# The first root's scaling of the rows on GpSimd instead of VectorE, in a two-layer RWKV-7 / HGRN2 trunk

## The reference, cut to what matters

```
x = x + rms_norm(out, norm_post[0])        # out: RWKV's output projection
h = rms_norm(x, norm_pre[1])
q, f_logit, i, z = split(h @ w_in, 4)      # HGRN2's input projection

def rms_norm(x, w):
    return x * rsqrt(mean(x * x, axis=-1) + NORM_EPS) * w
```

## Time and profile before

| | us |
|---|---|
| median of three runs | 2852.39 |
| lowest, highest | 2851.09, 2854.86 |
| profiled execution, its own time | 2853.62 |
| its span in the trace | 2851.8 |
| PE busy | 2730.1 |
| DVE busy | 1608.9 |
| ACT busy | 1259.1 |
| POOL busy | 138.4 |

### The profile page before, as it was taken

One profiled execution on the slowest core, in us unless ns is written; L12 is line 12 of the kernel. 1 busy time (PEld: TensorE's weight loads), 2 busy tenths in 40 slices (PEclk: granted clock), 3 DMA queues, 4 the chain that ended last, 5 costly groups with the idle time before them and its releaser, 6 DMA issues. The chain is left out here.

```text
span 2851.8 us, 82517 instructions
## 1 busy us (share of the span) xinstructions
PE 2730.1 (96%) x36816; PEld 2567.6 (90%) x36816; DVE 1608.9 (56%) x2679; ACT 1259.1 (44%) x1869; POOL 138.4 (5%) x116
## 2 busy tenths in 40 slices
PE   6999999999999999999889988999999999999997
PEld 5899999999998887888779978999999999999997
DVE  7335313313326777888742267776777767775224
ACT  5345323324414555555532255444544455444222
POOL 0000000000001111010000003000000000000000
PEclk8999999999999999999999999999999999999999
DMA  3333333333311111112132242222333223243322
GB/s 126 108 106 113 109 113 113 113 111 134 115 69 52 50 53 54 51 53 71 43 111 89 90 155 73 95 95 94 97 100 107 95 80 114 95 139 137 124 89 102
DMA packets 86816, 273.48 MB, mean 96 GB/s; under 512 B 16448, under 2 KB 29504, under 8 KB 65984
## 3 DMA queue, kind: packets, MB, share of 16 engines
q1 hardware_dynamic: 77248, 250.37, 26.5%
q10 hardware_dynamic: 9216, 17.83, 1.7%
HBM read 221.63 MB, written 46.54 MB: 94 GB/s over the span
## 5 line engine op out<-in xcount | busy, mean ns | idle before, releaser
L136 PE MATMUL w_pair<-a_x_hi,keep_w_hi 128*128 128x272 f32 x2016 | 428.4, 294 | 19.3 <-DVE a_x_lo L1059 18.5
L136 PE MATMUL w_pair<-a_x_lo,keep_w_hi 128*128 128x272 f32 x2016 | 419.7, 289 | 0.0
L136 PE MATMUL w_pair<-a_x_hi,keep_w_lo 128*128 128x272 f32 x2016 | 417.4, 288 | 0.0
L1045 DVE TENSOR_TENSOR keep_w_lo<-keep_raw,keep_w_hi 128x2048 fp32r<-128x2048 f32 x63 | 144.4, 2293 | 469.5 <-ACT keep_w_hi L798 469.5
L136 PEld LDWEIGHTS w_pair<-a_x_hi,keep_w_hi 128*128 128x128 f32 x2016 | 320.2, 189 | 25.7 <-issue 20.7
L136 PEld LDWEIGHTS w_pair<-a_x_lo,keep_w_hi 128*128 128x128 f32 x2016 | 318.1, 189 | 0.0
L136 PEld LDWEIGHTS w_pair<-a_x_hi,keep_w_lo 128*128 128x128 f32 x2016 | 317.8, 189 | 0.0
L136 PE MATMUL t_pair<-t_x_hi,keep_w_hi 128*128 128x272 f32 x1216 | 262.0, 297 | 18.2 <-DVE t_x_lo L2421 9.1
L136 PE MATMUL t_pair<-t_x_lo,keep_w_hi 128*128 128x272 f32 x1216 | 253.5, 290 | 0.0
L136 PE MATMUL t_pair<-t_x_hi,keep_w_lo 128*128 128x272 f32 x1216 | 253.3, 290 | 0.0
L812 ACT ACTIVATE a_stage<-w_pair 128x544 f32<-128x544 f32 x64 | 40.0, 625 | 425.1 <-PE w_pair L136 425.1
(11 more groups left out here) (448 smaller groups left out, 6146.7 us busy)
## 6 DMA issues: line engine op xcount, KB each, us to landing
keep_raw<-in_w_in SPq DMA_DIRECT2D x64, 1024.0 KB, 5.0
keep_raw<-in_hgrn_in SPq DMA_DIRECT2D x64, 1024.0 KB, 5.1
keep_raw<-in_rwkv_wo SPq DMA_DIRECT2D x16, 1024.0 KB, 5.0
keep_raw<-in_hgrn_wo SPq DMA_DIRECT2D x16, 1024.0 KB, 5.0
t_Ss<-in_hgrn_s SPq DMA_DIRECT2D x16, 512.0 KB, 7.1
out_hgrn_s<-t_Sd SPq DMA_DIRECT2D x16, 512.0 KB, 8.5
scr_r<-a_stage ACTq DMA_DIRECT2D x16, 272.0 KB, 2.2
scr_k<-a_stage ACTq DMA_DIRECT2D x16, 272.0 KB, 2.1
```

Of the source, the lines that this page charges most:

```text
L136: mm = pe.matmul(out[:, a, 0:TH], w, x[:, kt, a * TH:(a + 1) * TH], start=(kt == order[0] and n == 0), stop=(kt == order[-1] and n == 2))
L1045: dve.tensor_tensor(w_lo[b][:, :], raw[n % 2][:, :], w_hi[b][:, :].bitcast(F32), ALU.subtract).then_inc(p.raw_lo, 1)
```

## The change

The function `normed` moves from DVE's block to GpSimd's, with the same waits, operands and semaphore. GpSimd executes all sixteen after its memsets and ahead of the wait for the constants. DVE's loop keeps addition and low part.

```diff
@@ block.gpsimd
             for t in (A, Dg, As):
                 pool.memset(t[:, :], 0.0).then_inc(s.zeroed, 1)
+
+            def normed(kt):
+                pool.wait_ge(s.rstd, 1)
+                pool.wait_ge(s.evac, kt + 1)
+                pool.tensor_tensor(o[:, kt, :], o[:, kt, :], rstd[:, :], ALU.mult).then_inc(s.t, 1)
+
+            for kt in range(KT):
+                normed(kt)
             pool.wait_ge(s.const_in, 16 * len(names))
@@ block.vector
-            def normed(r, kt, g):
-                dve.wait_ge(s.rstd, 1)
-                dve.wait_ge(s.evac, g + kt + 1)
-                dve.tensor_tensor(o[:, kt, :], o[:, kt, :], rstd[:, :], ALU.mult).then_inc(s.t, 1)
@@
             for kt in range(KT + 1):
-                if kt < KT:
-                    normed(0, kt, 0)
-                if 1 <= kt <= KT:
+                if kt:
                     low_part(KT, kt - 1, "pre1")
                 if kt < KT:
                     dve.wait_ge(x_in[kt], 16)
                     dve.wait_ge(s.t, kt + 1)
                     dve.tensor_tensor(o[:, kt, :], o[:, kt, :], x_row[kt], ALU.add).then_inc(s.x1, 1)
```

## The result

The changed kernel takes 2858.61 us (median of 16 runs), the kernel before 2852.23 us (16 runs beside them). One run of the kernel before took 4744.5 us, was slow, and is not in the ratio. The ratio is 1.0026 with a 95% interval of 1.0018 to 1.0034, or 7.4 us with 5.1 to 9.7. The forecast was +10.7 us, 2863.1, with a range of 2857.5 to 2868: the time lies in the range, 1.1 us above its lower end, and the +10.7 themselves lie above the interval.

A forecast was written before the change was run, and what follows sets the result against it. PE, busy 96%, was taken as the bound, losing time only where it waits for x_lo. Turns of products, additions and x_lo delay row 7's x_lo by 10.7 us: 2852.39 + 10.7 = 2863.1 us, range 2857.5 to 2868.

The forecast's parts named there:

- turns instead of durations: DVE and GpSimd alternate, one instruction each, so costs are priced by turn; a row takes 3.71 us instead of 2.25.
- no exclusion: Rival: products and additions run beside each other, only the first row is 0.65 us later; 2853.0 us; chance 0.10.
- DVE keeps its turn: Rival: GpSimd gets in only between addition and x_lo, a row takes 2.47 us; about +3.5 us, 2855.9; chance 0.08.
- The order at the start: GpSimd starts with the root, and its first two products come before DVE's first addition.
- The terms of the sum: Sixteen product turns, eight addition turns, seven x_lo turns and row 7 undisturbed put row 7's x_lo 10.7 us later.
- The product's turn: One GpSimd product of 128x544 takes a turn of 1.24 us, with bounds of 0.95 and 1.54.
- The turn of x_lo: DVE's x_lo takes a turn of 0.65 us, against 0.58 for an addition.
- The pace before: In the kernel before, addition, x_hi and x_lo fill the 2.25 us from row 0's x_lo to row 1's.
- nothing comes back behind row 7: From row 8 PE's 2.48 us a row bind as before and everything behind keeps its distance, so 10.7 us stay.
- Nothing won on DVE: Removing sixteen scalings, 11.5 us of DVE's work, gains nothing after the first row: they lie in x_hi's shadow.
- The late clock: Rival: PE's pauses in rows 0 to 5 keep the clock at 0.50 when row 6 arrives; 2867 us; chance 0.08.

The follow-up runs named there:

- dummy: Kernel before, DVE still scaling all rows, plus sixteen GpSimd products of a 128x512 tile into scratch from the root on; ratio 1.0033 to the kernel before.
- copies: Kernel before, DVE still scaling all rows, plus twenty-four GpSimd copies of a 128x512 tile into scratch from the root on; ratio 1.0018 to the kernel before.
- fills: Kernel before, DVE still scaling all rows, plus thirty-two GpSimd memsets of a 128x512 tile from the root on; ratio 0.9995 to the kernel before.
- paced: Changed kernel, but GpSimd's product of each row waits for DVE's addition of the row before; ratio 1.0003 to the kernel before.

## Why the prediction was right, and where its size was off

The step that carried it was **turns instead of durations**, read from the earlier trace rows, and it held: every DVE instruction of the first seven rows is held up until a product ends, in alternation, even where DVE has two in a row. "dummy", "copies" and "fills" show that it is this and not the dependency, and they show it in the timed ratios too. The rival "no exclusion" (0.10) falls with the rows of 3.56 us, and so does "DVE keeps its turn" (2.47 us a row).

**The order at the start** was as forecast: two products go ahead of the first addition, which ends 3.27 us behind the root.

**The terms of the sum** were a little too large. The product's turn was put at 1.24 us and is 1.78 - 0.58 = 1.20. The Trainium skill's 2.6 cycles ("GPSIMD Engine Reference", section 3.1) had given an estimate of 1.18; this trace agrees within 0.02. For the products of "dummy" the same figure would give an estimate of 512 x 2.6 / 1200 = 1.11 us, and there the trace has 0.90. The turn of x_lo was put at 0.65 and is 0.58 like the addition's (1657.52 to 1658.10 in "paced"): the 0.06 us by which it is longer alone lie outside its turn. Together 16 x 0.04 + 7 x 0.07 = 1.1 us, so 9.6 instead of 10.7, and 29.84 - 20.18 = 9.66 was measured at row 7.

**The pace before** was read from one row, and the chain of three steps was called what fills the 2.25 us. That holds in six of the first seven steps; row 3 came 3.51 us behind row 2, through PE's first token sum, as "fills" showed. The sum has no term for it. It came out all the same, since it goes from the root to row 7 by absolute times: the 1.26 us are in the 1677.21 before, and after the change the 3.56 us of a row cover that wait (ScalarE's wait for the sum is 1.06 us there, and x_hi waits for the addition behind it). Counted by rows, 7 x 1.32 us and 1.69 us for the first x_lo make 10.9, less 1.3. That the sum needed no term here was luck, as the prediction never looked at row 3.

**That nothing comes back behind row 7** holds for the passage (9.66 becomes 9.45), and up to 908 us behind the passage all kernels stay together within 0.6 us. For the whole span it holds only up to the spread outside: the timed 7.4 and 8.3 us are below 9.5, whose ratio of 1.0033 lies inside both intervals. The prediction had no term for that spread, so of the 3.3 us between 10.7 and 7.4 only 1.1 are explained by the terms. Whether 1 to 2 us are given back outside the passage is open.

**Nothing won on DVE** was right: its busy time is unchanged (1608.9 and 1608.2 us), since being held up counts as busy and takes the place of the scalings. **The late clock** did not decide: PE's pauses in rows 0 to 5 did not keep the clock down, and it was at 1.00 when row 6 came.

## What to carry to other kernels

Work moved from DVE to GpSimd costs what its turns take from DVE where GpSimd runs ahead, and its whole duration only where DVE's next step stands behind it, when both read SBUF as here. Look first whether the removed step lay in a shadow (here 0.64 us under a wait of 0.82, worth nothing), then let the moved one run only where DVE waits anyway: in the passage the same sixteen products cost 9.5 us when they run ahead, 4.9 when paced by the additions, and eight of them in the PE-bound rows 1.4. Measure such a change by a stretch of the trace between two fixed events; it repeats within 0.3 us where the whole kernel before went from 2843.0 to 2855.0. But such a stretch is not the whole time, as "paced" shows. And look at every row of a loop, not at one: row 3 had another bound than its neighbours.

## What the runs showed of the hardware that I had not expected

- A GpSimd copy with one SBUF operand takes turns with DVE as well: 0.47 us for 512 columns, with DVE's instructions at 1.12 instead of 0.72. Memsets beside them change nothing (0.72 and 0.79). All these DVE instructions read two SBUF operands; one that reads a single operand was not tried.
- The turn of a GpSimd product is not the same for all products of a size: 0.90 us for 512 columns of a tile with itself and 0.89 in the earlier trace rows, but 1.20 for 544 columns of two different dense tiles, 1.13 if scaled to 512. Which property of the operands makes the difference was not tried.
- The granted clock can drop to half in a stretch in which PE is busy throughout, in one execution and not in another of the same kernel: 0.58 and 0.57 in two windows of 4 us, for 3.4 us of time.
